# Four RMS norms split into their gain, applied to the turned block, and their root, applied to the product

## The chip, the cores and the metric

One Trainium2 chip, one of its cores. A time is device time in microseconds (us) for one launch of the whole program. The kernel before was timed three times: 2165.26, 2167.34 and 2168.16 us, median 2167.34. The profile is one further execution, recorded instruction by instruction.

The engines by their names in the profile: PE is the matrix engine (PEld its weight loads), DVE the vector engine, ACT the scalar engine, POOL the engine that here takes roots and issues indirect transfers, SP the one that issues most of the weight loads. Each engine runs its own list in order and waits for the others on semaphores. A float32 matmul goes through PE in two passes, so a matmul of the code is two in the profile's counts.

## What is computed

256 tokens of width 1024 pass through three layers. The parts that matter here:

```python
def rms_norm(x, g):
    y = x * lax.rsqrt(mean(x * x, axis=-1) + EPS)
    return y * g

# first block
h = rms_norm(x, norm_attn);  proj = h @ w_in            # then MLA and dilated attention
x = x + merged @ w_out
h2 = rms_norm(x, norm_ffn)
gp = softmax(h2 @ w_rg + b_rg)                          # 4 groups, the best one
el = h2 @ w_re + b_re                                   # 8 experts of it, the best two
x = x + sum(combine[e] * (silu(h2 @ w_gate[e]) * (h2 @ w_up[e])) @ w_down[e])   # 32 experts

# second block, layer 0 (layer 1 has a convolution in the place of the attention)
x = x + attn_retention_mixer(rmsnorm(x, norm_mix[0]), even_w_in, even_w_out)
t = rmsnorm(x, norm_ffn[0])
# peer: 8 heads, top 16 of 128 x 128 pairs of keys, per token 128 rows u and v of a table
s = (t @ w_q) . sub_keys;  x = x + sum_k gate_k * gelu(t . u[e_k]) * v[e_k]
```

Because a norm's root is one number per token and its gain one number per column of x, `rms_norm(x, g) @ W` equals `root * ((x * g) @ W)`.

## The kernel before, in words

Tokens lie in two chunks c of 128, one token per partition: `x[:, c, :]`, and normed in `xn[:, c, :]`. PE needs the width on the partitions, so a chunk is turned: eight 128x128 transposes into two banks of 512 columns (k = 0 and k = 4), each copied out to `hT`, k = 0 by ACT and k = 4 by DVE. A product is eight matmuls of 512 columns into one bank, four for each weight tile of 1 MiB. Weight tiles go through a ring of six slots, and later through places in the arena too; SP issues each load when the slot's last tile is used.

A norm takes four engines in turn: ACT squares and sums x (L394), DVE makes the mean (L398), POOL the root (L402), DVE multiplies x by root and gain in two halves (L417). Only then can PE turn the chunk (L360).

The program in order, with the places that the change touches:

1. **Start.** SP fetches both chunks of x and the identity, ACT the gain (512 KB, broadcast to all partitions). PE runs six filler matmuls on zeros (`pe_idle_work`, L369), turns chunk 0, runs four fillers, and begins `w_in` (L345, L314). The first attention stage follows.
2. **Residual and router** (`pe_residual`, `dve_residual`, `act_residual`, `vector_moe`). Four half products of 512 columns with `w_out` (L455): chunk 0, chunk 0, chunk 1, chunk 1. Chunk 0 is normed and turned beside the third half, chunk 1 after the fourth. `router` (L1412) multiplies a turned chunk by 36 router columns; `choose(c)` is a chain of small DVE instructions (L1492 to L1533) that ends in `Ms(c)`, the tokens' two experts as ones; a matmul with a triangle (L1434, L1439) ranks the tokens of each expert; `whose_tile` and `whose_place` make a table, and DVE writes the rows' numbers (`to_rows`, L1585, L1587). ACT stores the normed rows in `h_rows` (L1682). POOL gathers them by that table (L1348).
3. **Experts.** Sixteen tiles, six weight tiles of 1 MiB each; 19 places hold weights in advance. Each place is loaded again when PE has used it (L1205).
4. **Even layer.** DVE adds the experts' rows to x (L1673), the chunk is normed (`mix0`), turned, and multiplied by seven slabs of 512 columns (L1824) in the order 0, 512, 1536, 2048, 1024, 2560, 3072, with attention and retention between them, then by `even_w_out` (L1915). This is chunk 0; four slabs of chunk 1 follow, the rest of it lies inside the next stage.
5. **Peer stages.** Chunk 0 is normed (`ffn20`), turned and scored (L2334), DVE chooses the first head's 16 rows, and POOL issues 512 indirect gathers (L2818) of 128 rows of 8 KB, five ahead of their use. DVE takes the dot product of each (L2716), ACT makes a diagonal matrix of its weights (L2783), and PE adds the second half of the rows through it (L2702). The rest of chunk 1's even layer, the odd layer, and all later norms are spread between these positions by a table of positions.

## Time and profile before

| what | us |
|---|---|
| median of three runs | 2167.34 |
| lowest, highest | 2165.26, 2168.16 |
| the profiled execution: its span, first to last instruction | 2168.7 |
| PE busy in it | 1855.1 |
| DVE busy | 1305.5 |
| POOL busy | 687.5 |
| ACT busy | 493.1 |

The page gives no time for the profiled execution beside its span. The span lies 1.4 us above the median and 0.5 us above the highest of the runs. Differences of stages are read inside the span and taken off the median.

In the page's second part each digit is the busy share of one fortieth of the span (54 us), in tenths. PE is busy nearly everywhere in the first third. The DMA engines are busy from slice 8 on, except in slices 11 and 13, which hold the change from the experts to the even layer and the beginning of the peer stage.

### The profile page before, as it was taken

The page shows a single profiled execution, that of the slowest core. Times are in us where ns is not written, and L with a number is a line of the kernel's source. Part 1 is how long each engine was busy: PE and PEld are TensorE (multiplying, and loading weights), DVE is VectorE, ACT ScalarE, POOL GpSimd, SP SyncE. Part 2 cuts the span into 40 slices and gives each one's busy share as a digit, 9 for nine tenths or more (in the row PEclk, how much of TensorE's full clock was granted, in tenths as well). Part 3 has the DMA queues.
Part 4 walks back from the last instruction along what each step waited for, and adds up shares of the span by engine and source line. Part 5 has one row for each costly group of instructions (what it writes and reads, how often), then busy time and mean ns, then how long its engine had stood idle before and what let it go on. Part 6 is the DMA issues. An engine that isn't in the chain of part 4 may idle for free.

```text
span 2168.7 us, 19290 instructions
## 1 busy us (share of the span) xinstructions
PE 1855.1 (86%) x5992; PEld 893.5 (41%) x5992; DVE 1305.5 (60%) x3327; ACT 493.1 (23%) x1232; POOL 687.5 (32%) x593
## 2 busy tenths in 40 slices
PE   9999999998799989999877787777888767878875
PEld 4445555333245445455433333333433433434332
DVE  1343433221033668667587797987777898777764
ACT  1232221111022233222221122222212222222221
POOL 2110001111000334344343344453434444444442
PEclk9999999999999999999998998889999988999999
DMA  7432367999795999999999999999999999999996
GB/s 250 168 122 81 128 271 249 415 418 419 293 385 201 395 390 374 422 420 421 421 422 421 420 399 415 422 416 421 421 421 421 392 409 416 422 421 421 421 410 259
DMA packets 115081, 781.44 MB, mean 360 GB/s; under 512 B 16080, under 2 KB 17792, under 8 KB 21664
## 3 DMA queue, kind: packets, MB, share of 16 engines
q0 software_dynamic: 78928, 542.37, 60.9%
q1 hardware_dynamic: 32544, 227.75, 26.4%
q10 hardware_dynamic: 3504, 10.04, 1.2%
q8 instruction: 50, 0.82, 0.2%
q14 instruction: 55, 0.45, 0.1%
HBM read 782.20 MB, written 10.49 MB: 366 GB/s over the span
## 4 chain that ended last, share of the span: by engine, by line
DMA 29%; DVE 17%; issue 14%; POOL 6%; PE 5%; ACT 0%; POOLq 0%; DVEq 0%; ACTq 0%
DMA arena<-in_c_rows_dram,arena 29%; DVE arena L2716 7%; POOL arena L2818 6%; PE banks L1824 2%; DVE x L2726 2%; PE banks L2702 1%; DVE arena L2610 1%; DVE arena L2613 1%; DVE arena L2619 1%; PE banks L1915 1%; DVE arena L2648 1%; DVE arena L2652 0%; DVE arena L2577 0%; DVE small L2607 0%; DVE xn L417 0%
## 5 line engine op out<-in xcount | busy, mean ns | idle before, releaser
L2702 PE MATMUL banks<-arena 128*128 128x512 f32 x1784 | 885.4, 642 | 240.0 <-ACT arena L2783 239.1
L2818 POOL DMA_INDIRECT arena<-in_c_rows_dram,arena x512 | 609.7, 1191 | 817.5 <-PE banks L2702 571.3
L2716 DVE CUSTOM_DVE_ANT_0 arena<-arena,xn 128x1024 f32<-128x1024 f32 x512 | 625.4, 1223 | 296.9 <-DMA arena<-in_c_rows_dram,arena 294.2
L2702 PEld LDWEIGHTS banks<-arena 128*128 128x128 f32 x1784 | 345.8, 203 | 714.2 <-issue 356.6
L2783 ACT ACTIVATE arena<-ident,small 128x128 f32<-128x128 f32 x446 | 158.2, 395 | 536.6 <-DVE small L2723 524.7
L314 PE MATMUL banks<-ring,hT 128*128 128x512 f32 (+1 forms) x480 | 202.2, 577 | 0.0
L376 ACT COPY arena<-banks 128x512 f32<-128x512 f32 (+4 forms) x218 | 101.2, 493 | 292.5 <-PE banks L360 112.7
L2774 ACT ACTIVATE small<-small 128x2 f32<-128x2 f32 x256 | 52.1, 204 | 499.1 <-DVE small L2716 498.9
L402 POOL TENSOR_TENSOR small<-small 128x1 f32<-128x1 f32 (+4 forms) x24 | 33.5, 1398 | 303.3 <-DVE small L398 276.9
L314 PEld LDWEIGHTS banks<-ring,hT 128*128 128x128 f32 x480 | 87.9, 191 | 100.1 <-issue 98.4
L2407 PE MATMUL banks<-ring,hT 128*128 128x512 f32 x176 | 88.3, 606 | 0.0
L2726 DVE SCALAR_TENSOR_TENSOR x<-arena,small,x 128x1024 f32<-128x1024 f32 x66 | 84.9, 1286 | 2.4
L381 DVE COPY arena<-banks 128x512 f32<-128x512 f32 (+1 forms) x35 | 23.6, 675 | 96.4 <-PE banks L1269 67.4
L2450 PEld LDWEIGHTS banks<-hT,ring 128*128 128x128 f32 x448 | 62.5, 197 | 33.4 <-issue 33.4
L1250 PE MATMUL banks<-arena 128*64 128x512 f32 x280 | 71.6, 596 | 2.9 <-DMA arena<-in_c_experts_dram 2.9
L1362 POOL DMA_INDIRECT y_rows<-arena x16 | 16.0, 1001 | 183.0 <-ACT arena L376 99.8
L1327 DVE TENSOR_TENSOR arena<-arena,banks 128x256 f32<-128x256 f32 x16 | 6.7, 422 | 103.9 <-ACT arena L1299 103.9
L1824 PE MATMUL banks<-ring,hT 128*128 128x512 f32 x144 | 63.6, 592 | 0.0
L2450 PE MATMUL banks<-hT,ring 128*128 128x128 f32 x448 | 62.9, 280 | 0.0
L360 PEld LDWEIGHTS banks<-ident,arena 128*128 128x128 f32 (+1 forms) x416 | 47.3, 140 | 31.1 <-issue 28.3
L610 DVE SCALAR_TENSOR_TENSOR arena<-arena,banks 128x128 f32<-128x128 f32 (+1 forms) x64 | 19.7, 350 | 66.0 <-PE banks L554 66.0
L360 PE MATMUL banks<-ident,arena 128*128 128x128 f32 (+1 forms) x416 | 55.3, 275 | 2.1 <-DVE arena L1327 1.5
(319 smaller groups left out, 1805.3 us busy)
## 6 DMA issues: line engine op xcount, KB each, us to landing
arena<-in_c_experts_dram SPq DMA_DIRECT2D x51, 1024.0 KB, 21.5
ring<-in_c_w_in_dram SPq DMA_DIRECT2D x30, 1024.0 KB, 4.8
ring<-in_c_experts_dram SPq DMA_DIRECT2D x30, 1024.0 KB, 24.9
ring<-in_c_odd_w_in_dram SPq DMA_DIRECT2D x19, 1024.0 KB, 9.8
ring<-in_c_w_q_dram SPq DMA_DIRECT2D x18, 1024.0 KB, 9.6
ring<-in_c_even_w_in_dram SPq DMA_DIRECT2D x12, 1024.0 KB, 19.2
arena<-in_c_even_w_in_dram SPq DMA_DIRECT2D x10, 1024.0 KB, 15.4
arena<-in_c_rows_dram,arena POOLq DMA_INDIRECT x512
```

The costliest lines, as they stand in the source:

```text
L314: r = e.matmul(banks[:, b, 0:n], lhs[:, k + i, c * P:(c + 1) * P], wt[:, i, :], start=(k + i == 0), stop=(k + i == kn - 1))
L360: r = e.transpose(banks[0:m, b, i * P:(i + 1) * P], s, ident[:, :])
L376: e.copy(dst, src).then_inc(ac.sem, ac.up(name))
L1250: r = e.matmul(banks[H * h:H * h + H, b, :], gT[:, n % 2, 4 * part + k, H * h:H * h + H], wt[h][:, k, :], start=(part == 0 and k == 0), st ...
L1824: r = e.matmul(banks[:, bank_of[name], :], hT[:, k + i, c * P:(c + 1) * P], wt[:, i, :], start=(k + i == 0), stop=(k + i == 7))
L2407: r = e.matmul(banks[:, bank_of[name], :], hT[:, k, c * P:(c + 1) * P], wt[:, k % 4, :], start=(k == 0), stop=(k == 7))
L2450: r = e.matmul(banks[:, bank_of[name], f * P:(f + 1) * P], wt[:, k, f * P:(f + 1) * P], hT[:, k, c * P:(c + 1) * P], start=(k == 0), stop= ...
L2702: r = e.matmul(banks[:, bank_of[("acc", L, c, hf)], :], diag[:, diag_of[m], :], rows[:, row_of[m], D + hf * 512:D + (hf + 1) * 512], start ...
L2716: e.tensor_tensor_reduce(u, u, xn[:, c, :], 1.0, 0.0, ALU.mult, ALU.add, hid3[:, c, h, k:k + 1]).then_inc(ve.sem, ve.up(("u", p)))
L2726: e.scalar_tensor_tensor(x[:, c, :], rows[:, row_of[p - 1], D:2 * D], hid3[:, c, h, k + 1:k + 2], x[:, c, :], ALU.mult, ALU.add).then_inc( ...
L2783: e.activation(diag[:, diag_of[m], :], ident[:, :], ACT.Copy, scale=hid3[:, c, h, k:k + 1]).then_inc(ac.sem, ac.up(("diag", m)))
L2818: e.indirect_dma_start(rows[:, b, :], None, table_uv, bass.IndirectOffsetOnAxis(ap=eix[:, c, 16 * h + k:16 * h + k + 1], axis=0)).then_inc ...
```

## The change

The norms `attn`, `ffn`, `mix0` and `ffn20` are split. Three later norms stay as they were.

- PE turns x itself (`pe_turn_half`). The gain lies in a small tensor, one column per block of 128 (`c_gains`, 16 KB), and is multiplied in while the turned block is copied out: one DVE instruction for four blocks with a broadcast (`dve_gained`), or four ACT instructions with a scale operand (`act_gained`).
- The root multiplies what comes out of the product, as a scale in ACT's copy (`act_rooted`) or in DVE's. The router's logits get it in `scalar_tensor_tensor`.
- In the residual stage chunk 0 is turned in the middle of the third half product, the router's first matmuls run before the fourth, `choose(0)`, its table and its rank run beside the fourth. The normed rows for `h_rows` are still needed: DVE multiplies x by the gain, ACT by the root.
- At the end of the experts the three fillers before the turn go. In the even layer the score of the first two heads stands ahead of chunk 1's first product, of which the first half stood ahead of the turn before.
- The identity is fetched before x, and the broadcast gains of `attn` and `mix0` are no longer fetched.

```diff
+        def pe_turn_half(e, n, c, k):
+            turn(e, ("hT", n, c, k), [x[:, c, (k + i) * P:(k + i + 1) * P] for i in range(4)])
+        def act_gained(e, n, c, k):
...
+            for i in range(4):
+                e.activation(hT[:, k + i, c * P:(c + 1) * P], banks[:, bank_of[name], i * P:(i + 1) * P], ACT.Copy,
+                             scale=gain_T[n][:, k + i:k + i + 1]).then_inc(ac.sem, ac.up(name))
+        def dve_gained(e, n, c, k):
...
+            e.tensor_tensor(hT[:, k:k + 4, c * P:(c + 1) * P], turned(name, P, 4),
+                            gain_T[n][:, k:k + 4].unsqueeze(2).to_broadcast([P, 4, P]),
+                            ALU.mult).then_inc(ve.sem, ve.up(name))
+        def await_root(e, n, c):
+            e.wait_ge(po.sem, po.at(("ms", n, c)))
+        def act_rooted(e, name, dst, src, n, c):
+            await_root(e, n, c)
+            e.wait_ge(pe.sem, pe.at(name))
+            e.activation(dst, src, ACT.Copy, scale=ssn[n][:, c:c + 1]).then_inc(ac.sem, ac.up(name))
...
-            a2 = half(1, 0)
+            a2 = half(1, 0, first_turned)
             rings.drop(a2)
-            pe_turn_chunk(e, n, 0, xn[:, 0, :])
-            mid0(e)
-            a3 = half(1, 512)
-            mid1(e)
+            router(e, 0)
+            a3 = half(1, 512, ranked)
             rings.drop(a3)
-            pe_turn_chunk(e, n, 1, xn[:, 1, :])
+            turn_added(e, 1, 0)
+            turn_added(e, 1, 4)
+            router(e, 1)
...
+            def square(c):
+                e.wait_ge(ve.sem, ve.at(("res" + n, 512, "c", c)))
+                e.activation(scratch, x[:, c, :], ACT.Square,
+                             accum_out=ssn[n][:, c:c + 1]).then_inc(ac.sem, ac.up(("sq", n, c)))
+            def normed(c):
+                await_root(e, n, c)
+                e.wait_ge(ve.sem, ve.at(("xg", n, c)))
+                e.activation(xn[:, c, :], xn[:, c, :], ACT.Copy,
+                             scale=ssn[n][:, c:c + 1]).then_inc(ac.sem, ac.up(("xn", n, c)))
+                store(e, c)
             e.wait_ge(ve.sem, ve.at(("res" + n, 512, "c", 0)))
             free(e)
+            square(0)
+            act_gained(e, n, 0, 0)
+            normed(0)
+            act_gained(e, n, 1, 0)
+            chain(e, ac)
+            square(1)
+            normed(1)
...
         def vector_first(e):
             e.memset(hT[:, 0:2, :], 0.0).then_inc(ve.sem, ve.up("zeros"))
+            e.wait_ge(pe.sem, pe.at(("idle", "x")))
+            dve_gained(e, "attn", 0, 0)
             for c in range(2):
-                dve_norm(e, "attn", c)
-            for c in range(2):
-                dve_turned_chunk(e, "attn", c)
+                e.wait_ge(ac.sem, ac.at(("sq", "attn", c)))
+                dve_mean(e, ssn["attn"][:, c:c + 1], D, ("ms", "attn", c))
+            dve_gained(e, "attn", 1, 0)
...
-                step(e.tensor_tensor(g8[:, 0:4], banks[:, b, 0:4], rb[:, 0:4], ALU.add))
-                step(e.tensor_tensor(l, banks[:, b, 4:36], rb[:, 4:36], ALU.add))
+                step(e.scalar_tensor_tensor(g8[:, 0:4], banks[:, b, 0:4], root, rb[:, 0:4], ALU.mult, ALU.add))
+                step(e.scalar_tensor_tensor(l, banks[:, b, 4:36], root, rb[:, 4:36], ALU.mult, ALU.add))
...
-            await_hT(e, "mix0", 1)
-            pe_even_in(e, 1, 0, 0)
-            pe_turn_chunk(e, "ffn20", 0, xn[:, 0, :])
+            for c0, k in ((0, 0), (512, 4)):
+                e.wait_ge(ve.sem, ve.at(("joined", 0, c0)))
+                pe_turn_half(e, "ffn20", 0, k)
             await_hT(e, "ffn20", 0)
             pe_score(e, 0, 0, (0,))
             pe_score(e, 0, 1, (0,))
-            pe_even_in(e, 1, 0, 4)
+            e.wait_ge(ve.sem, ve.at(("hT", "mix0", 1, 0)))
+            e.wait_ge(ac.sem, ac.at(("hT", "mix0", 1, 4)))
+            both(1, 0)
             both(1, 512)
...
             for i in range(2):
                 e.wait_ge(ys_out[i].sem, ys_out[i].at("all"))
             pe_idle_work(e, "results", 8, still)
-            e.wait_ge(ve.sem, ve.at(("x", "mix0", 0)))
-            pe_idle_work(e, "results added", 3, still)
             tensor_even(e)
```

On PE the residual and router stage, before. The matmuls on `ring,hT` are the half products, those on `small,hT` the router, those on `small` alone fillers; the last row is the first rank.

```order
L455 MATMUL banks<-ring,hT 128x512 x16
L360 MATMUL banks<-ident,xn 128x128 x8
L455 MATMUL banks<-ring,hT 128x512 x8
L1412 MATMUL banks<-small,hT 128x36 x8
L369 MATMUL banks<-small 128x288 x4
L360 MATMUL banks<-ident,xn 128x128 x8
L1412 MATMUL banks<-small,hT 128x36 x8
L1434 MATMUL banks<-arena,small 128x32
```

The same place on PE in the changed kernel:

```order
L490 MATMUL banks<-ring,hT 128x512 x12
L361 MATMUL banks<-ident,x 128x128 x8
L490 MATMUL banks<-ring,hT 128x512 x4
L1489 MATMUL banks<-small,hT 128x36 x8
L490 MATMUL banks<-ring,hT 128x512 x4
L1503 MATMUL banks<-arena,small 128x32
L490 MATMUL banks<-ring,hT 128x512 x4
L361 MATMUL banks<-ident,x 128x128 x8
L1489 MATMUL banks<-small,hT 128x36 x8
```

The turn moved into the third half product, the router ahead of the fourth, the rank into its middle, and the four fillers are gone.

On PE the change from the even layer's chunk 0 to the scores, before. L1915 is the last product of chunk 0, L1824 are chunk 1's products, L2334 the queries and L2346 their scores.

```order
L1915 MATMUL banks<-arena,hT 128x512 x8
L1824 MATMUL banks<-arena,hT 128x512 x4
L360 MATMUL banks<-ident,xn 128x128 x8
L2334 MATMUL banks<-hT,arena 128x128 x16
L2346 MATMUL banks<-arena 128x128 x2
L2334 MATMUL banks<-hT,arena 128x128 x16
L2346 MATMUL banks<-arena 128x128 x2
L1824 MATMUL banks<-arena,hT 128x512 x28
```

And in the changed kernel:

```order
L1985 MATMUL banks<-arena,hT 128x512 x8
L361 MATMUL banks<-ident,x 128x128 x8
L2412 MATMUL banks<-hT,arena 128x128 x16
L2424 MATMUL banks<-arena 128x128 x2
L2412 MATMUL banks<-hT,arena 128x128 x16
L2424 MATMUL banks<-arena 128x128 x2
L1894 MATMUL banks<-arena,hT 128x512 x32
```

Four matmuls of chunk 1 moved from before the turn to behind the scores.

## Rows read from the trace of the kernel before

**Rows 1.** The page: busy tenths of the DMA engines in 40 slices.
```profile
DMA  7432367999795999999999999999999999999996
```

**Rows 2.** Instructions in time, start: start us, us, engine, line, operation.
```profile
1.46 7.43 PE L369 MATMUL banks<-hT 128*128 128x512 f32 x12 [1.46 <-DVE hT L910]
...
11.17 1.02 PE L345 MATMUL banks<-ring,hT 128*128 128x512 f32 x2
```

**Rows 3.** Longest wait of PE from 15 to 325 us: total, times, longest.
```profile
PE banks L554 <- ACT arena L376: 1.8, 2, 1.0
```

**Rows 4.** Instructions in time, router stage.
```profile
345.97 1.87 PE L1412 MATMUL banks<-small,hT 128*128 128x36 f32 x16
...
348.31 0.56 POOL L402 TENSOR_TENSOR small<-small 128x1 f32<-128x1 f32 x1 [14.06 <-DVE small L398]
...
350.47 0.34 ACTq L1682 DMA_DIRECT2D h_rows<-xn  x1
...
354.32 0.16 DVE L1492 TENSOR_TENSOR arena<-banks,small 128x4 f32<-128x4 f32 x1
...
357.32 0.19 DVE L1533 TENSOR_TENSOR arena<-arena 128x32 f32<-128x32 f32 x1
...
362.42 0.17 DVE L1587 TENSOR_SCALAR arena<-arena 128x16 uint32<-128x16 uint32 x1
...
363.52 1.17 POOL L1348 DMA_INDIRECT arena<-h_rows,arena  x1 [14.66 <-issue]
...
369.10 1.04 PE L360 MATMUL banks<-ident,arena 128*128 128x128 f32 x8
```

**Rows 5.** Line L1682, the stores of h_rows.
```profile
DMA to landing us min/median/max: 6.8/7.0/7.3
```

**Rows 6.** Line L1348, the gathers of h_rows, 360 to 372 us.
```profile
DMA to landing us min/median/max: 3.3/3.5/3.7
```

**Rows 7.** Stretches: us, engines busy, granted clock, DMA share, GB/s.
```profile
360.00:365.00 5.00, 3.86 (x10) 3.04 (x11) 1.60 (x14) 1.45 (x8) 1.17 (x2) 0.55 0.91 374
370.00:375.00 5.00, 5.00 (x30) 2.41 (x30) 0.69 (x1) 0.32 (x1) 0.99 (x1) 1.00 0.09 26
500.00:510.00 10.00, 7.10 (x30) 2.55 (x27) 1.09 (x2) 1.06 (x3) 0.00 (x0) 0.83 1.02 418
720.00:740.00 20.00, 18.16 (x43) 7.83 (x42) 19.00 (x55) 6.63 (x15) 6.99 (x6) 1.00 1.01 418
```

**Rows 8.** Instructions in time, beginning of the even layer.
```profile
606.72 1.06 ACT L394 ACTIVATE xn<-x 128x1024 f32<-128x1024 f32 x1 [15.76 <-DVE x L1673]
...
611.88 3.60 PE L1824 MATMUL banks<-ring,hT 128*128 128x512 f32 x8
```

**Rows 9.** The chain that ended last, even layer: slab 1024 of chunk 0.
```profile
642.96 6.87 PE banks L1824 x16
```

**Rows 10.** Line L275, issues of SP from 608 to 608.7 us.
```profile
L275 SPq DMA_DIRECT2D ring<-in_c_even_w_in_dram x2: 446/570/695, 607.8 to 608.6; - x2
...
DMA to landing us min/median/max: 12.2/12.2/12.2
```

**Rows 11.** Line L275, issues of SP from 610.4 to 611 us.
```profile
L275 SPq DMA_DIRECT2D arena<-in_c_even_w_out_dram x2: 442/463/484, 610.1 to 610.6; - x2
...
DMA to landing us min/median/max: 23.3/23.3/23.3
```

**Rows 12.** Instructions in time, beginning of the peer stage.
```profile
683.31 0.69 DVE L2042 TENSOR_TENSOR x<-x,banks 128x512 f32<-128x512 f32 x1 [2.74 <-PE banks L1915]
...
689.05 3.81 PE L2334 MATMUL banks<-hT,arena 128*128 128x128 f32 x32 [0.83 <-ACT hT L376]
...
705.66 1.03 POOL L2818 DMA_INDIRECT arena<-in_c_rows_dram,arena  x1 [19.67 <-DVE arena L2668]
...
716.87 1.22 DVE L2716 CUSTOM_DVE_ANT_0 arena<-arena,xn 128x1024 f32<-128x1024 f32 x1 [3.02 <-DMA arena<-in_c_rows_dram,arena]
```

**Rows 13.** Instructions in time: a pair of 128x128 ACTIVATEs with a scale operand.
```profile
740.51 0.69 ACT L2783 ACTIVATE arena<-ident,small 128x128 f32<-128x128 f32 x2 [1.14 <-DVE small L2723]
```

More of the change, by code:

```diff
@@ L442, in sp_residual, with pe_residual, half @@
                     load(e, ("res" + n, c0, k), w[c0 // 256 + k // 4])
-        def pe_residual(e, n, lhs, second, mid0, mid1, ready):
-            def half(c, c0):
+        def pe_residual(e, n, lhs, second, ready, router, ranked):
+            def half(c, c0, between=None):
                 name = ("res" + n, c0, "c", c)
@@ L483, in add, with times_gain, mean @@
                 emptied[name] = (ve.sem, ve.n)
+            def times_gain(c, c0):
+                g = fetched("gain_" + n)
+                e.wait_ge(g.sem, g.at("all"))
+                chain(e, ve)
+                e.tensor_tensor(xn[:, c, c0:c0 + 512], x[:, c, c0:c0 + 512], gain[:, gain_of[n], c0:c0 + 512],
+                                ALU.mult).then_inc(ve.sem, ve.up(("xg", n, c)))
+            def mean(c):
+                e.wait_ge(ac.sem, ac.at(("sq", n, c)))
+                dve_mean(e, ssn[n][:, c:c + 1], D, ("ms", n, c))
@@ L494, in dve_residual, with act_residual @@
-            mid1(e)
-            dve_turned_chunk(e, n, 1)
-        def act_residual(e, n, mid0, mid1, free):
+            dve_gained(e, n, 1, 4)
+            mean(1)
+            times_gain(1, 512)
+        def act_residual(e, n, store, free):
+            def square(c):
[8 more added lines that the diff above has]
+                store(e, c)
@@ L1006, in scalar_first @@
         def scalar_first(e):
-            gain_fetch(e, "attn")
+            g = fetched("gains")
+            e.dma_start(gT_all, a["c_gains"]).then_inc(g.sem, g.up("all", by=16))
             for c in range(2):
@@ L1414, in router @@
                 r.then_inc(pe.sem, pe.up(("lg", c)))
-            def first_router(e):
-                router(e, 0)
-                pe_idle_work(e, "norm", 4, still)
-            still = rw.rearrange("p k n -> p (k n)")
-            pe_residual(e, "ffn", hT, second, nothing, first_router, ready)
-            router(e, 1)
-            rings.drop(("lg", 0))
-            rings.drop(("lg", 1))
             def bank(name):
@@ L1428, in bank, with ranked @@
                 return b
-            b = bank(("rank", 0))
-            e.wait_ge(fetched("tri").sem, fetched("tri").at("all"))
-            e.wait_ge(po.sem, po.at("ones"))
-            e.wait_ge(ve.sem, ve.at(("Ms", 0)))
-            e.matmul(banks[:, b, 0:32], tri, Ms[:, 0, :], start=True, stop=True).then_inc(pe.sem, pe.up(("rank", 0)))
+            def ranked(e):
+                b = bank(("rank", 0))
+                e.wait_ge(fetched("tri").sem, fetched("tri").at("all"))
+                e.wait_ge(po.sem, po.at("ones"))
+                e.wait_ge(ve.sem, ve.at(("Ms", 0)))
+                e.matmul(banks[:, b, 0:32], tri, Ms[:, 0, :], start=True, stop=True).then_inc(pe.sem, pe.up(("rank", 0)))
+            still = rw.rearrange("p k n -> p (k n)")
+            pe_residual(e, "ffn", hT, second, ready, router, ranked)
+            rings.drop(("lg", 0))
+            rings.drop(("lg", 1))
             b = bank(("rank", 1))
@@ L1561, in whose_place, with chosen @@
                                          ALU.is_equal, ALU.mult), ("hots", c))
-            first = choose(0)
-            def some(n):
-                for _ in range(n):
-                    next(first, None)
-            dve_residual(e, "ffn", lambda e: some(3), lambda e: some(5))
-            for _ in first:
-                pass
-            e.wait_ge(po.sem, po.at("ids"))
-            whose_tile(0)
+            def chosen(e):
+                for _ in choose(0):
+                    pass
+                e.wait_ge(po.sem, po.at("ids"))
+                whose_tile(0)
+            dve_residual(e, "ffn", chosen, lambda e: whose_place(0))
             for _ in choose(1):
                 pass
-            whose_place(0)
             whose_tile(1)
@@ L2105, in scalar_even @@
         def scalar_even(e):
[L2106 removed]
+            act_gained(e, "mix0", 1, 4)
             past(e, "moe", pe, ve, po)
```

130 lines of the change are left out of this document (80 added, 50 removed).

## The prediction, made before the change was run

> **What bounds the kernel now.** I read the page first. Its DMA line [rows 1] shows the transfers busy from slice 8 to the end but for slices 11 and 13, so the experts and the peer stages run at the pace of the transfers, and the first attention stage, slices 1 to 6, does not. The list of waits, asked for PE from 15 to 325 us, has nothing longer than 1.8 us in all [rows 3]: the first stage runs at the pace of PE, and what its beginning gains is kept. Then the instructions in time at the four norms. What one of them gives depends on what comes due behind it, so each is followed until a transfer or PE takes over.
>
> **The start.** PE works at fillers until 1.46 + 7.43 = 8.89 us and begins the first product at 11.17 [rows 2]. Now x itself is turned, so PE turns as soon as the fillers end, and no earlier, since they stay. Eight transposes take at most 1.04 us, the last row of [rows 4], the four small fillers behind them as much, and the copy-out is beside these. The product starts at 10.6 to 11.0: 0.2 to 0.5 us gained, I take 0.4. ACT's half as four instructions costs more than one copy: a pair takes 0.69 [rows 13], so four some 1.3 us against 0.6, but PE needs that half only after the first half's product. The identity ahead of x costs nothing, since x is now awaited until 8.9. POOL's small transfers are issued later, because the mean of chunk 1 waits behind DVE's and ACT's turned blocks. I price that at nothing: they first serve angles and the small norms, while PE works off products, and what they delay at most is DVE, not PE.
>
> **The router.** Before, the fourth half product ends at 345.97, where the router begins [rows 4]. Now the router of chunk 0 (1.87, but for its overlap 1.7) and the rank (0.3) come ahead of that end: 348.1. `Ms(0)` must be there when PE has done the first half of the fourth product. The chain from L1492 to L1533 takes 3.2 us (354.32 to 357.51) and the four matmuls 3.4, so PE stalls 0.2 at most. What is queued behind that wait is the rest of the product, and behind it all of chunk 1. From 348.1: DVE adds (0.69, as in rows 12), ACT copies the turned block out in four, until 350.1, then squares (1.06 plus reading its sum, 1.25), mean and root take 0.9 (POOL's part 0.56), so the root is there at 352.2, and the router's product at about 352.0. `choose(1)` starts at 352.3 instead of 354.32. The chain of it is 3.2 again, and the whole of chunk 0's table, 1.2 us of `whose_place`, no longer stands behind it. The table's numbers were ready at 362.42 + 0.17 = 362.6; now at about 359.1, 3.5 earlier.
>
> That gain isn't all kept. The store of chunk 1's rows was issued at 350.47 [rows 4] and is now behind the square, the root and a multiplication by ACT (about 1.1): 353.4. Stores took 6.8 to 7.3 us to land [rows 5], so 360.2 to 360.7, later than the table. The first gather follows 0.9 behind the later of both (as 363.52 behind 362.6), at 361.3, and lands after 3.3 to 3.7 [rows 6], at 364.8. The two loads that wait for the same store are issued with it and share the transfers; I add 0.4. Before, the first gather landed at 363.52 + 3.7 = 367.2, but PE turned its rows only at 369.10: it was at its nine fillers, at a clock of 0.55 [rows 7]. If the clock is low there again, PE is free at 366.3 (359.1 and the same 7.2 us), if not at 365.2. I take 366.0, 3.1 us gained. The ends are 2.0 (POOL's 363.52 against 361.3, less some contention) and 3.9. From here on the gain is kept: at 370 to 375 the transfers stand still (share 0.09) until PE frees the first place, then run at a share of 1.02 (500 to 510 us) [rows 7] to the end of the experts.
>
> On the contention the Trainium skill ("DMA: Bandwidth & Descriptors", Queues, rings and completion order) says that a DMA engine takes packets from its queues in turn. By that the gather does not stand behind 2 MiB of weights; behind them it would come about 5 us later, and this norm would lose 1 to 2 us. The trace agrees with taking turns: the store issued at 350.47 landed within 7.3 us with a load of 1 MiB issued just ahead.
>
> **The even layer's beginning.** x is complete where ACT begins its square, 606.72, and the first product begins at 611.88 [rows 8], 5.2 us later. Now: turn 1.04, four small fillers 1.04, so 608.8, 3.1 earlier; the turn of chunk 1 waits for no norm, which gives 0.7 more. The removed 512 KB of gain and the three fillers are only room. But this is lost again at slab 1024. Its tile is the twelfth that SP asks for after the experts' results have landed. The fourth, issued at 607.8, landed 12.2 us later, 620.0 [rows 10], the ninth, issued at 610.6, 23.3 us later, 633.9 [rows 11]: 2.8 us a tile, so the twelfth lands at about 642.2 (an estimate). PE uses it at 642.96 [rows 9]. The transfers do not start earlier relative to the results, so of 3.8 us only 0.3 to 0.8 is left; I take 0.5. PE then stands still there for about 3 us.
>
> **The scores.** From the end of the last product of chunk 0 (683.1) to the first query matmul (689.05) [rows 12] are 5.9 us, 3.4 of them covered by a product of chunk 1. Now the wait is DVE's add (0.7 + 0.2), a half turned (0.6) and ACT's or DVE's copy-out (0.9): 2.5 us. The choice of the first rows and the first gather (705.66) come 3.4 us earlier, and 3.9 with the tile's 0.5. But the covering product, 3.4 us, is now behind the scores, so all later products of chunk 1 come only 0.5 earlier, and with them three things: the slots that the second to fifth gathers wait for, and the loads that wait for the same slots. From 720 to 740 the transfers have a share of 1.01 and DVE works 19 of 20 us [rows 7]. DVE's first dot product (716.87) may come 3 us earlier, the following ones wait for their rows. I give this stage 0.3 more than PE's shift. The bounds are 0 and 3.4. Scale operands in later ACT copies cost some 0.1 us each on an engine that is a quarter busy, and count nothing.
>
> **Sum.** 0.4 + 3.1 + 0.5 + 0.3 = 4.3 us off the span of 2168.7, and as much off the median of the runs, 2167.34: 2163.0. The likeliest case's own range is 2161 to 2165.
>
> **Rivals.**
> - *The choice decides the peer stage.* The critical chain goes through the first gather and DVE (716.87 is on it). If these decide, and not transfers and PE, the end moves by all 3.9: 0.4 + 3.1 + 3.9 = 7.4, 2160.0. For it: DVE is at 95%. Against: the transfers' 1.01 in the same stretch.
> - *The clock.* The new wait ahead of slab 1024 is 3 us. In the experts' stage PE waits for weights, and the granted clock is 0.83 from 500 to 510, which is 1.7 us of PE lost [rows 7]. If PE falls to its lower level (1.2 GHz) there and again between the turn and the scores, 2 x 1.7 = 3.4 are lost: 2166.4. The Trainium skill ("TensorE: Matmul & The Clock Gate", Why this matters for your kernels) advises against idle gaps between bursts of matmuls for this reason, and so speaks against taking out the fillers; by it this case would be the likely one. The trace is of two minds: it shows the low clock after such waits, but also at 360 to 365 among fillers.
> - *The router's gain is hidden.* The store lands as late as it can and the gather behind the loads: 1 us left of 3.1: 2165.1.
> - *Slower: the peer stage meets another phase.* From 740 to 860 PE, DVE and transfers are all near their limits and take turns in waiting. The product that moved behind the scores makes PE the one that frees the slots late, and each late slot keeps a gather back. The place is the first three heads of chunk 0; the price is 3.4 us of PE, twice if the scores of the next heads come late as well. It decides once more than 4.3 us of transfer time stands empty there in addition: 6.8 - 4.3, 2169.9.
>
> **Numbers.** What a measurement of this kernel tells from no change is about 0.2%, 4.3 us, so the forecast lies on the edge. Chances: forecast 0.42 (half of it below 2163.0), choice 0.18, clock 0.15, router hidden 0.15, slower 0.10. Faster by over 0.2%: 0.21 + 0.18 and the parts of the others in which two gains meet (the first stage's clock can differ by 1.7 as well), 0.11: 0.50. Within 0.2%: 0.42. Slower by over 0.2%, above 2171.7: only the last rival at its worst, 0.08. The range leaves out the far end of the last two: 2158.5 to 2167.5.
>
> **What would show it.** The first product at 10.6 to 11.0. `Ms(0)` there when the fourth product is half done; the first gather of h_rows behind the store's landing, not behind the table; PE turning its rows about 3 us earlier. A wait of PE for a transfer ahead of slab 1024, which the profile before does not have. The first query matmul about 4 us earlier, chunk 1's products about 0.5 (all counted beyond the router's 3.5). I am wrong if slab 1024 finds its tile there, if the gather waits for the table, or if from 860 us on the peer positions are earlier by more than 6 or less than 3 us.

## The result and the profile after: slower by 0.19%, where 0.2% faster was forecast

| kernel | median us | runs | ratio to before, 95% interval |
|---|---|---|---|
| before | 2167.36 | 20 | |
| changed | 2170.60 | 20 | 1.0019, 1.0010 to 1.0027 |

The forecast was 2163.0, within 2158.5 to 2167.5. The changed kernel lies 3.2 us above the kernel before by the medians (0.15%), outside the range and on the other side.

The profiled execution of the changed kernel has a span of 2165.7 us; its run took 2167.46, near the low end of the 20 (2166.74 to 2179.34). That of before, 2168.7, lies above the median of its kernel: in every recorded run the time is about 1.8 us longer than the span, so it stands for about 2170.5 (an estimate). One pair of profiles therefore says the opposite of 20 runs of each kernel, and the places below are read from several profiles of each.

The start, instructions in time, changed kernel (against [rows 2]):

```profile
1.46 7.32 PE L370 MATMUL banks<-hT 128*128 128x512 f32 x12 [1.46 <-DVE hT L980]
...
8.61 1.04 PE L361 MATMUL banks<-ident,x 128*128 128x128 f32 x8
...
10.38 3.60 PE L346 MATMUL banks<-ring,hT 128*128 128x512 f32 x8
```

The turn follows the fillers at once and the first product is 0.79 us earlier in this profile.

The router stage (against [rows 4]; L1489 is the router, L1567 the beginning of `choose`, L1657 the last of the table's numbers, L1755 the store of h_rows, L1282 SP's loads of experts' weights, L1425 the gather, L361 the turn):

```profile
344.27 3.68 PE L490 MATMUL banks<-ring,hT 128*128 128x512 f32 x8
...
351.90 0.22 DVE L1567 SCALAR_TENSOR_TENSOR arena<-banks,small 128x4 f32<-128x4 f32 x1
...
353.07 0.33 ACTq L1755 DMA_DIRECT2D h_rows<-xn  x1
...
358.72 0.18 DVE L1657 TENSOR_SCALAR arena<-arena 128x16 uint32<-128x16 uint32 x1
358.94 0.33 SPq L1282 DMA_DIRECT2D hT<-in_c_experts_dram  x1
359.39 0.36 SPq L1282 DMA_DIRECT2D xn<-in_c_experts_dram  x1
359.82 1.17 POOL L1425 DMA_INDIRECT arena<-h_rows,arena  x1 [8.19 <-DMA h_rows<-xn]
...
367.42 1.09 PE L361 MATMUL banks<-ident,arena 128*128 128x128 f32 x8 [1.83 <-DMA arena<-h_rows,arena]
```

Everything up to the gather's issue is as early as forecast or earlier: `choose(1)` at 351.9 (forecast 352.3), the table at 358.9 (359.1), the gather at 359.82 (361.3), 3.7 us before that of [rows 4]. The store of h_rows took 5.9 us here, not 6.8 to 7.3 [rows 5]: it landed at 358.9 too, so the gather did not stand behind the store as forecast. Then it takes 7.6 us until PE can turn the rows, and PE waits for them.

What moved meanwhile, from two answers on the DMA queues of the changed kernel, 360 to 363.9 us and 364 to 368 (packets, MB, share of the 16 engines; q1 carries SP's loads, q0 POOL's gathers):

```profile
q1 hardware_dynamic: 183, 1.37, 90.5%
```
```profile
q1 hardware_dynamic: 92, 0.62, 37.7%
q0 software_dynamic: 432, 0.48, 33.7%
```

For 4.3 us after the gather's issue no packet of it moves; SP's two loads, issued 0.9 and 0.4 us ahead of it, do. In the profile before the first packet moved 1.7 us after the issue, so 2.6 us of the 4.3 are new. In [rows 4] the two loads were issued at 357.81 and 358.63, 5 us ahead of the gather, which then landed in 3.3 to 3.7 us [rows 6].

The even layer's beginning (ACT's loads of the experts' results, L1772 here, then SP's loads of weights, which wait for them). Before, with the product of slab 1024:

```profile
599.07 0.82 ACTq L1700 DMA_DIRECT2D arena<-y_rows  x2
...
606.41 2.60 SPq L275 DMA_DIRECT2D ring<-in_c_even_w_in_dram  x5
...
642.79 7.03 PE L1824 MATMUL banks<-ring,hT 128*128 128x512 f32 x16
```

Changed:

```profile
595.47 0.81 ACTq L1772 DMA_DIRECT2D arena<-y_rows  x2
...
604.09 2.46 SPq L276 DMA_DIRECT2D ring<-in_c_even_w_in_dram  x5
...
606.34 3.60 PE L1894 MATMUL banks<-ring,hT 128*128 128x512 f32 x8
...
639.25 7.39 PE L1894 MATMUL banks<-ring,hT 128*128 128x512 f32 x16 [1.36 <-DMA ring<-in_c_even_w_in_dram]
...
652.58 3.70 PE L1894 MATMUL banks<-ring,hT 128*128 128x512 f32 x8 [1.19 <-DMA ring<-in_c_even_w_in_dram]
```

The first product is 5.5 us earlier than in [rows 8]: 3.6 come from the result loads, which are issued that much earlier, and 1.9 are gained between the two, where the forecast had 3.1. From the issue of the result loads to SP's first load behind them it takes 8.6 us where it took 7.3, and PE waits for weights twice, at slab 1024 as forecast and again in slab 2560. From the issue of the result loads to the end of chunk 0's last join it takes 86.1 us, before 84.2.

The second profile of the changed kernel (`e1_after`, see below) looks different at slab 1024. The first row is its product, the second the stretch from 642 to 645 us (us, engines busy, granted clock, DMA share, GB/s); the third is the same stretch of before:

```profile
640.62 8.80 PE L1894 MATMUL banks<-ring,hT 128*128 128x512 f32 x16 [2.91 <-DMA ring<-in_c_even_w_in_dram]
```
```profile
642.00:645.00 3.00, 3.00 (x5) 1.28 (x4) 1.48 (x4) 0.00 (x0) 0.00 (x0) 0.51 1.00 410
```
```profile
642.00:645.00 3.00, 3.00 (x15) 1.80 (x14) 1.80 (x4) 2.22 (x4) 0.00 (x0) 1.00 1.01 412
```

After a wait of 2.9 us PE runs this product for 3.4 us at its lower level, 1.2 GHz, and needs 8.80 us for it instead of 7.03.

### The profile page after: what moved, and what is told of

It reads as the page before. It is cut to its first block, busy times and chain, and to the rows that moved or that the text cites. A ratio compares the mean times of both kernels' runs of the same rounds, so it can differ in the third digit from the quotient of the medians.

```text
span 2165.7 us, 19328 instructions
## 1 busy us (share of the span) xinstructions
PE 1844.2 (85%) x5978; PEld 887.9 (41%) x5978; DVE 1301.6 (60%) x3320; ACT 503.0 (23%) x1254; POOL 678.6 (31%) x593
## 4 chain that ended last, share of the span: by engine, by line
DMA 33%; DVE 15%; issue 13%; POOL 5%; PE 5%; ACT 0%; POOLq 0%; DVEq 0%; ACTq 0%
DMA arena<-in_c_rows_dram,arena 32%; DVE arena L2796 7%; POOL arena L2898 5%; DVE x L2806 2%; DMA ring<-in_c_even_w_in_dram 1%; PE banks L2782 1%; PE banks L1894 1%; DVE arena L2690 1%; DVE arena L2693 1%; PE banks L370 1%; DVE arena L2699 1%; PE banks L2412 1%; PE banks L1985 1%; DVE arena L2728 1%; DVE arena L2732 1%
## 5 line engine op out<-in xcount | busy, mean ns | idle before, releaser
L2898 POOL DMA_INDIRECT arena<-in_c_rows_dram,arena x512 | 600.8, 1173 | 826.5 <-PE banks L2782 544.0
L377 ACT COPY arena<-banks 128x512 f32<-128x512 f32 (+4 forms) x185 | 83.6, 478 | 191.9 <-PE banks L361 111.6
L382 DVE COPY arena<-banks 128x512 f32<-128x512 f32 x32 | 22.1, 690 | 86.5 <-PE banks L1346 66.4
L361 PEld LDWEIGHTS banks<-ident,arena 128*128 128x128 f32 (+1 forms) x416 | 47.1, 140 | 34.5 <-issue 26.9
L361 PE MATMUL banks<-ident,arena 128*128 128x128 f32 (+1 forms) x416 | 55.5, 275 | 5.0 <-DMA arena<-h_rows,arena 1.8
```

What stands on the lines that cost most here:

```text
L361: r = e.transpose(banks[0:m, b, i * P:(i + 1) * P], s, ident[:, :])
L377: e.copy(dst, src).then_inc(ac.sem, ac.up(name))
L2898: e.indirect_dma_start(rows[:, b, :], None, table_uv, bass.IndirectOffsetOnAxis(ap=eix[:, c, 16 * h + k:16 * h + k + 1], axis=0)).then_inc ...
```

## Where the time lies, over all profiles

Each experiment below was profiled too, and most share their code with one of the two kernels at the places that matter. So each place can be read several times. Shifts are us against the first profile of before (negative is earlier). The dot products are counted from 0, and the place is the beginning of number 48.

| stretch | text before | text changed |
|---|---|---|
| the restart: the experts' first load behind the gathers | 0, -0.3, 0.0 | -1.6, -1.6, -0.7, -0.1, -2.6, +0.6, +1.1, -1.9: mean -0.9 |
| result loads to the last join, us | 84.2, 84.3, 84.2 | 86.1, 86.6, 86.7, 86.5, 86.6, 86.6: +2.3 |
| last join to first query matmul, us | 5.8 | 2.3: -3.4 |
| first query to dot product 48, us | 175.2, 171.3, 172.5 | 175.6, 176.5, 176.7: +3.3 |
| dot product 48 to the end, us | 1304.5, 1304.8, 1304.6 | 1306.2, 1304.5, 1306.9: +1.2 |

The sum, -0.9 + 2.3 - 3.4 + 3.3 + 1.2, is +2.5; the medians of the 20 runs differ by 3.2. About 0.7 us has no place in this table. Two limits of it: the first row takes eight profiles and the last three rows only three, whose spans alone are 1.1 us longer on the mean than the three of before; and over all twelve profiles with the split of `mix0` the last row is +0.6 rather than +1.2.

The row from the result loads to the last join hides two things that come and go:

- *A packet of PE's instructions among the results' last packets.* In the seven profiles that have one 5.0 to 5.7 us after ACT's issue, SP's first load follows that issue by 8.6 to 8.8 us. In the eleven others it follows by 7.3 to 7.5.
- *The clock at slab 1024.* PE waits there in all twelve profiles with the split of `mix0`, and in none of the six without it. In eight of the twelve the clock then falls to its lower level for 3.4 us and the product takes 8.6 to 8.8 us instead of 7.0 to 7.4. Whether it falls is not settled by the length of the wait: it fell after 2.0 us and did not after 2.65.

| | clock falls at slab 1024 | it does not |
|---|---|---|
| packet among the results | 86.5, 86.6, 86.6, 86.6 | 86.1, 86.7 (a second wait, in slab 2560); 84.3 (ACT's loads later) |
| no packet | 85.7, 85.7, 85.5, 85.8 | 84.0 |

The numbers are us from the result loads to the last join; without the split it is 84.2 or 84.3 in all six. ACT's loads are later in the 84.0 too and in the last three of the left lower cell. So the fall of the clock costs about 1.7 us (85.7 against 84.0), and the packet 0.8 to 0.9 beside it (86.5 and 86.6 against 85.7). The second wait is long only where the clock doesn't fall and PE is at slab 2560 sooner.

## The experiments

**The kernels again, and parts undone.** `e1_before` and `e1_after` are the two kernels unchanged. `e1_noS` takes the norm `ffn20` and its order back; its core:

```diff
-            for c0, k in ((0, 0), (512, 4)):
-                e.wait_ge(ve.sem, ve.at(("joined", 0, c0)))
-                pe_turn_half(e, "ffn20", 0, k)
+            pe_even_in(e, 1, 0, 0)
+            pe_turn_chunk(e, "ffn20", 0, xn[:, 0, :])
```

`e1_onlyF` is the kernel before with the diff's `pe_residual`, `dve_residual`, `act_residual`, `choose` and what they call, and nothing else.

> The kernel before, unchanged, for a second profile. All theories: its median within 2 us of 2167.4. If the spread of its runs comes from the peer stage, then its 160th dot product lies elsewhere than 1194.3 us, by up to 3 us, while the join of the even layer ends at 683.1 within 0.5.

> The changed kernel, unchanged, for a second profile: 2170.6 within 2 us. Theory 'lost in the peer stage': its query matmul at 683.9 as in the first profile, and the 16th to 160th dot products later than in that one by 2 to 6 us. Theory 'lost earlier': the query matmul itself comes later than 683.9 by 2 us or more in a typical run.

> The changed kernel with the norm ffn20 and the order around its turn as before (the first half product of chunk 1 ahead of the turn, norm, turn, scores). Theory 'the product that moved behind the scores puts the peer stage into a worse phase': 2165 to 2167, 4 to 6 below the changed kernel. Theory 'the loss comes from another norm': within 1.5 of the changed kernel, 2169 to 2172.

> The kernel before with the split of ffn and the reordered router alone; attn, mix0 and ffn20 as before. Theory 'the router gain is real and kept': 2164 to 2166, 1.7 to 3 below before. Theory 'the router is where it is lost' (the experts' transfers or the clock in them): 2169 to 2171.

Measured: before 2168.92 (12 runs, ratio 0.9998 to 1.0024), changed 2169.70 (1.0001 to 1.0023), without the split of `ffn20` 2170.91 (1.0008 to 1.0030), router alone 2168.37 (0.9991 to 1.0012). Undoing `ffn20` gives nothing back, so the loss isn't the product that moved behind the scores; the router alone gains nothing that can be measured. The first query of the changed kernel, at 683.9 in its first profile, is at 685.5 in the second and 686.8 in the third (`e4_after`): the first profile was early there. The second profile of before differs from the first by 3.8 us at the end and by 0.3 at the join: its gain lies between the first gather and dot product 48, so a peer stage alone varies by that much with one text.

**Three causes, one edit each, and all together.** In `e2_gather_first` SP's loads into hT and xn also wait for the first gather:

```diff
             elif s in (XN_AT, HT_AT):
+                e.wait_ge(xg_in[0].sem, xg_in[0].at(("xg", 0)))
                 e.wait_ge(fetched("h_rows").sem, fetched("h_rows").at("all"))
```

In `e2_code_moved` the fillers behind the experts are `[still] * 4 + [still[:, 0:P]] * 16` instead of eight `still`. In `e2_act_later` four loads, the two gains and those of kt and cw, move in ACT's program:

```diff
-            gain_fetch(e, "ffn20")
-            gain_fetch(e, "mix1")
-            g = fetched("kt0")
...
             act_even_out(e, 0, 2560)
+            gain_fetch(e, "ffn20")
+            gain_fetch(e, "mix1")
+            g = fetched("kt0")
```

> The changed kernel, but SP's two 1 MiB loads that wait for the store of h_rows (into hT and xn) also wait until the first gather of h_rows has landed. Theory 'the gather stands behind these two loads': the first gather lands 3.3 to 3.7 us after its issue instead of 7.2 to 8.5, PE turns its rows 1.5 to 2.5 us earlier relative to the gather's issue, the stretch after it is at full clock, and everything behind is 1.5 to 3 us earlier: about 2168. Rival 'a gather issued within a microsecond of the table is slow by itself': the landing stays over 6 us and the time at 2170.

> The changed kernel, with the eight filler matmuls of 512 columns at the end of the experts as four of 512 and sixteen of 128 columns: same length, 48 instructions more on PE (with the weight loads), so that PE's next code packet (16 KB) is fetched earlier. Theory 'that packet holds up the last rows of the experts' results on one of the 16 DMA engines': the packet is fetched before 597 us, the second result load lands 7.3 us after its issue instead of 8.7, and the even layer's weights come 1.3 us earlier: 2169. Rival 'it lands late because nothing follows it in its queue': 8.7 stays, 2170.5.

> The changed kernel, with ACT's loads of two gains, the keys and the convolution (2.1 MB) issued behind its copy-out of slab 2560 instead of at the beginning of the even layer. Theory 'these loads, now issued 1 to 1.6 us earlier against the weights, take the share of slab 2560': the second tile of 2560 arrives up to 3 us earlier, PE's wait there goes and the last join of chunk 0 ends 1.5 to 2 us earlier against the results' arrival: 2168.5 if it is kept. Rival 'weights alone saturate the queues': no change, 2170.5.

> The three edits together. If they add: first gather landed within 3.7 us, results landed within 7.4, no wait at slab 2560, so the first query matmul is 4 to 6 us earlier than in the changed kernel. If the peer stage passes on what comes before it: 2165. If it gives none of it on (the transfers decide from there): 2170.

Measured, 12 runs each, against before: gather first 2164.51 (0.9976 to 0.9999); code moved 2167.43 (0.9994 to 1.0015); ACT later 2168.90 (0.9995 to 1.0019); all three 2162.13 (0.9971 to 0.9996).

With the gather first, line L1426, 355 to 372 us, and the instructions there:

```profile
DMA to landing us min/median/max: 3.3/4.5/7.2
```
```profile
359.87 1.17 POOL L1426 DMA_INDIRECT arena<-h_rows,arena  x1 [8.29 <-DMA h_rows<-xn]
...
363.27 0.33 SPq L1283 DMA_DIRECT2D hT<-in_c_experts_dram  x1
...
365.36 1.04 PE L361 MATMUL banks<-ident,arena 128*128 128x128 f32 x8
```

The first gather lands in 3.4 us, the loads then go out, and at the restart nothing is seen of their delay, since they only filled the gap that follows. The transfers of the experts start 3.7 us earlier than before instead of 0.9 on the mean, and 3.1 of it are left at the result loads. (In the same answer for the changed kernel, 358 to 368 us, the three values are 5.5, 6.3 and 7.6.) The time fell by more than the 3 us forecast, to 2164.5 where 2168 was expected; its profile, with a span of 2166.4, doesn't show where.

All profiles say the same of the gather. In the nine in which it goes out with the two loads its first packet moves 3.6 to 4.7 us after the issue and it lands after 7.2 to 9.5. In the nine in which it has 5 us of distance to them or goes first, these are 1.7 and 3.4 to 3.7. The rival, that a gather issued just behind the table is slow by itself, is out. What holds its packets back (the DMA engines, or the making of its descriptors) isn't shown.

PE's clock adds to it. Stretches (us, engines busy, granted clock, DMA share, GB/s) of `e4_noA`, a later run with the same router text, in which fillers ran at full clock, were done at 361 us and PE then waited 6.9 us for the gather; then of all three edits:

```profile
360.00:365.00 5.00, 1.31 (x6) 0.70 (x4) 0.00 (x0) 0.00 (x0) 2.00 (x2) 1.00 1.00 370
365.00:370.00 5.00, 1.76 (x8) 1.76 (x9) 0.00 (x0) 0.59 (x1) 0.00 (x0) 0.55 0.27 99
370.00:375.00 5.00, 5.00 (x25) 3.04 (x26) 0.69 (x1) 0.00 (x0) 0.99 (x1) 0.77 0.10 26
```
```profile
360.00:365.00 5.00, 4.34 (x29) 3.44 (x29) 0.69 (x1) 0.58 (x1) 2.79 (x4) 1.00 0.53 117
365.00:370.00 5.00, 5.00 (x24) 1.63 (x24) 0.00 (x0) 0.00 (x0) 0.56 (x1) 1.00 0.97 386
```

After the long wait PE turns the rows and does the first expert's products at its lower level, 1.2 GHz; the eight transposes take 1.97 us instead of 1.09. This is why an earlier gather could end in a later restart (+0.6, +1.1 us in the table): in the four profiles in which the clock is low for 6.8 us behind that wait, the restart is at -0.7, -0.1, +0.6 and +1.1; in the five others with the loads beside the gather, router alone among them, it is at -0.8 to -2.6. With all three edits together PE turned the rows at 361.5 to 362.9 at full clock in four profiles of four, and the restart came 6.1 to 7.5 us earlier than before. The fillers ran at full clock there and at the lower one in `e2_gather_first`; no edit aims at that, and why isn't known.

With the code moved, the queues' answers. First the changed kernel, 595.4 to 604.2 us, then `e2_code_moved`, 596.5 to 604.5 us:

```profile
q10 hardware_dynamic: 288, 2.10, 63.0%
q8 instruction: 1, 0.02, 0.7%
...
arena<-y_rows ACTq DMA_DIRECT2D x2, 1024.0 KB, 6.5
```
```profile
q10 hardware_dynamic: 288, 2.10, 69.1%
issues: line engine op xcount, KB each, median us to landing
arena<-y_rows ACTq DMA_DIRECT2D x2, 1024.0 KB, 5.8
```

One packet of instructions, 16 KB, runs from 601.2 to 602.2 us in the changed kernel. Fifteen of the sixteen last packets of the results have come by 602.3. A chain of three more packets of 8 KB begins at 602.2, where that of the instructions ends, and the sixteenth comes at 603.6; SP, which waits for it, issues at 604.09. Between the two almost nothing moves (DMA share 0.04):

```profile
602.20:603.40 1.20, 1.20 (x4) 0.50 (x3) 0.88 (x1) 0.00 (x0) 0.00 (x0) 1.00 0.04 14
```

In `e2_code_moved` the packet came at 595.8 and SP's loads began at 603.88, 7.3 us after ACT's at 596.59. In the kernel before it came at 613.5. To the last join it now took 85.7 us instead of 86.1 to 86.7, although the clock fell at slab 1024. The runs gained more than this 1 us explains (2167.4 against 2170.6), which the spread between series allows.

With ACT's loads later the second tile of slab 2560 lands 51.0 us after the issue of the result loads instead of 57.1, the wait there is gone, and the last join is back at 84.3 us after them, though the code packet is still there. But the clock did not fall in that profile. In three of the four with all edits it fell and the join came at 85.5 to 85.8, so the 84.3 isn't the edit's alone. The tile came at 51.0 in all of them. Nor was the earlier issue of ACT's loads enough to make it late: with the code moved they went out just as early (15.9 us after the result loads), and the tile came at 54.5, as in the kernel before (54.6). The profile of `e2_act_later` lost its gain again: it had the worst restart but one (+0.6) and 179.8 us from the query to dot product 48. So that this edit pays by itself isn't shown by its runs; that it removes the wait is.

**What the norms are worth.** `e3_noM` takes the split of `mix0` back in the changed kernel (the norm, its turn, the copies with a root, the three fillers). `e3_router_gather` is `e1_onlyF` with the edit of `e2_gather_first`. `e3_all_order` is all three edits with

```diff
+            pe_even_in(e, 1, 0, 0)
             for c0, k in ((0, 0), (512, 4)):
...
-            both(1, 0)
+            pe_even_in(e, 1, 0, 4)
```

and `e3_all_noS` all three edits with `ffn20` as in `e1_noS`.

> The changed kernel with the norm mix0 as before (gain fetched as one row, x multiplied by root and gain, three fillers ahead of the turn). Theory 'the split of mix0 costs more than it gives': from the issue of the result loads to the end of chunk 0's last join it takes 84.2 us as in the kernel before instead of 86.1 to 86.7, and the time is 1.5 to 2.5 below the changed kernel. Rival 'it costs nothing there': 86 or more, and the time as the changed kernel's.

> The kernel before with the split of ffn and the reordered router alone, and SP's two loads waiting for the first gather. Theory 'the router gives its 3 us once the gather is alone': the transfers of the experts start again 3 to 3.7 us earlier than in the kernel before, and the time is 3 to 4 below it, 2163 to 2164.5. Rival 'PE's fillers and its low clock keep it': 0 to 1.5 earlier, 2166 to 2167.

> All three edits, and the first half product of chunk 1 ahead of the turn and the scores again (the norm ffn20 stays split). Theory 'chunk 1's products and the transfers set the pace, not the scores': from the last join to the 48th dot product 178 to 180 us as with the scores first, time within 1.5 of 2162.5. Rival 'the scores first are worth their 3.4 us': 3 us slower.

> All three edits, with the norm ffn20 and the order around it as before. Theory 'the split of ffn20 is worth nothing': within 1.5 of 2162.5. Rival 'it is worth its 3.4 us once the stages ahead are mended': 2165 to 2166. Rival 'it costs': below 2161.

Measured: without the split of `mix0` 2169.13 (1.0008 to 1.0026), and 84.3 us to the last join, as expected; the code packet no longer falls into the result loads either. Only about 1 us of the 2.3 shows in the median. Router alone with the gather first 2166.85 (0.9986 to 1.0007): the experts' transfers start 3.1 us earlier, 3.1 are left at the result loads, and the stretch from the join to dot product 48 was 181.6 us instead of 177 to 181. The place is as the theory said, the time as the rival said. Product ahead of the scores again 2163.12 (0.9976 to 0.9997), 1.0 above the first result of all three and 2.6 above the second. From the join to dot product 48 it took 181.8 us, where 178 to 180 was expected and the two profiles of all three have 177.9 and 178.3. So the place speaks for a worth of 3.5 to 3.9 us and the time for less; one profile doesn't settle it. Without the split of `ffn20` 2165.04 (0.9985 to 1.0006): 2.9 above the first result of all three, while its profile, 2158.8, is the shortest of all. Between nothing and 3 us this isn't settled.

**One more series.**

> The kernel before, unchanged, in one series with the changed kernel. All theories: the experts' transfers start again within 0.3 us of the first profile's place, and from the issue of the result loads to the last join it takes 84.2 to 84.4 us. Theory 'the split as a whole costs about 1.5 us': 1 to 2 us faster than e4_after; theory 'it costs about 3': 2.5 to 4 faster.

> The changed kernel, unchanged, in one series with the kernel before. The experts' transfers start again between 2.6 earlier and 0.6 later than before, as in the five profiles of this router code so far; 86.1 to 86.7 us from the result loads to the last join; 5.2 minus 1.8 to 3 us at the first query matmul.

> The changed kernel with the norm attn and the start as before. Theory 'the start's 0.8 to 1 us is kept to the end of the attention stage, but lost at the gather, which is as late as the loads beside it make it': the router begins 0.8 to 1.2 us later than in the changed kernel, the transfers start again in the same band, and the time is within 1 of it. Rival 'the start is the part that pays': 1 us slower.

> The three edits together a second time, as the version that should beat both: 2161 to 2164, 3 to 5 below the kernel before of this series and 6 to 8 below the changed kernel. If its first result was luck: 2165 or more.

`e4_noA` has the diff's parts for the start undone. Measured: before 2166.82 (12 runs), changed 2172.16 (9 runs, ratio 1.0013 to 1.0033), without the split of `attn` 2171.35 (1.0004 to 1.0024), all three again 2160.50 (6 runs, 0.9957 to 0.9980). The last is the version that beats both kernels, by some 4 to 7 us the kernel before and 8 to 12 the changed one. Before and changed differ by 5.3 us here, more than either theory had (1 to 2, or 2.5 to 4), and by 0.8 in the first series: one series of 12 doesn't size this difference. The start's part makes no difference that can be measured; its router began 0.35 us later than in `e4_after`, not 0.8 to 1.2.

## Why the prediction was wrong, step by step

In the forecast's own terms the sum was 0.4 + 3.1 + 0.5 + 0.3 = 4.3 us gained. The router, with what was left of the start, gave 0.9 instead of 3.5, the even layer lost 2.3 instead of gaining 0.5, the scores gave about nothing, and the rest, which had no term, lost 0.6 to 1.2.

- **The start** was right at its place: the first product came 0.8 us earlier in the first profile, and over the twelve profiles with the new start 0.6 on the mean (9.9 to 11.3 against 11.2), where 0.4 was forecast. How much is kept isn't settled. Among the profiles with the changed router its matmuls of chunk 1 begin at 349.3 to 350.2 where the clock was low for 3.4 us at about 29 us, and at 348.2 to 349.0 where it was not. In the first group the new start is ahead by 0.6 us, in the second by nothing. "What its beginning gains is kept" is thus shown in part only.
- **The router** failed in one step: "lands after 3.3 to 3.7 [rows 6], at 364.8. The two loads that wait for the same store are issued with it and share the transfers; I add 0.4." PE turned the rows 7.2 to 9.6 us after the gather's issue in nine profiles (5.3 to 5.6 in three of before). [Rows 6] was taken at a moment when the two loads had been under way for 5 us; the change brought the gather and the loads together, and the loads won. So 3.3 to 3.7 plus 0.4 was mis-sized: the landing took 7.2 to 9.5. The rule of the Trainium skill that I set beside it ("DMA: Bandwidth & Descriptors", Queues, rings and completion order: a DMA engine takes packets from its queues in turn) is not what shows here: nothing of the gather moved for 3.6 to 4.7 us, where 1.7 is its own delay. The row I took as agreement was a store against a load, both issued by hardware queues, and says nothing on a gather. "About 5 us later", which I had written for the other case, is near what came (about 4 to 6 later). It was also the rival "The router's gain is hidden" (1 us left of 3.1), by its second half: the gather behind the loads, but not a late store. With the start's share taken off, even less was left on the mean.
- **The clock** was a rival with a chance of 0.15, and its first half came true: the wait ahead of slab 1024 was there in all twelve profiles with the split (forecast about 3 us), and in eight of them the clock fell behind it, at 1.7 us each, the price that I had given it. Of the changed kernel's own three profiles one shows the fall, of its variants seven of nine; the first profile, with 1.4 us of waiting and no fall, is not the usual case. The second half did not come: the clock stayed full between the turn and the scores. A further fall came behind the wait for the gather, a place where I had put PE at its fillers.
- **The even layer** failed in "The transfers do not start earlier relative to the results, so of 3.8 us only 0.3 to 0.8 is left; I take 0.5". The twelfth tile did land where I had put it, 43.3 to 44.2 us after the result loads in every profile (before 43.4), and PE used it 43.4 to 44.4 us after them, before 43.7 to 43.9: a gain of 0.4 at the most, and a loss of up to 0.6 in some. What failed is that I followed the stage no further than this tile, and left out the clock behind the wait. Three things came on top: the fall of the clock (1.7 us, in eight of twelve); SP's loads, which started 1.3 us later because the second result load landed later behind a packet of PE's instructions (0.8 to 0.9 at the join); and, where the clock did not fall, a second wait in slab 2560 (1.2 and 1.7 us), whose second tile landed 56.7 to 57.7 us after the result loads instead of 54.6. ACT's own loads, to which I gave no term, share the queues then: with four of them moved away the tile lands at 51.0. Instead of a gain of 0.5 there was a loss of 2.3.
- **The scores** were right: the query matmul 3.4 us earlier against the join, and chunk 1's products not. The change gains nothing there (0.3 forecast), since what was gained at the query is paid back up to dot product 48; with `ffn20` as before the query comes 5.8 us behind the join and that stretch takes 172.5 us, as in the third profile of before.
- **The rest**, to which I gave nothing, lost 0.6 to 1.2 us. What does it isn't known. I had written that I am wrong if from 860 us on the positions are not at least 3 us earlier: dot product 48 begins 0.1 us earlier on the mean of three profiles of each. The rival on the other side (the peer stage meets another phase, 3.4 us of PE, first three heads; its sum of 6.8 - 4.3 gives 2169.8, not 2169.9) names the right sign and nearly the time, but by luck: with that product put back, alone or on top of the three edits, the time does not fall.
- The forecast also leaned on one profile of before that was 3.0 and 3.8 us slower than the two others of the same text, nearly all of it in the peer stage. I noted the span against the median (1.4 us) and drew nothing from it.

## What to carry to other kernels

When a change brings a small transfer forward, list what else is issued at that new moment, above all what waits for the same signal; a landing time read where the small transfer was alone is a lower bound only. If the large loads only fill a gap, let them wait for the small one: here that one wait took the time from above the kernel before to just below it (2164.5 against 2166.4). Where a forecast puts a new wait on PE, give the clock behind it a term of its own. Where runs of one text differ by as much as the change, read each stretch from several profiles, relative to its own beginning, before explaining a total.

## What the runs showed that was not expected

- With two loads of 1 MiB issued 0.9 and 0.4 us ahead of an indirect gather of 128 rows no packet of it moved for 4.3 us, and it landed after 7.6; with the loads held back its first packet moved after 1.7 us and it landed after 3.4.
- PE's instructions are themselves fetched, 16 KB at a time, 50 times in the kernel, about 1 us each. One that falls into the last microseconds of a load delays its landing by 1.3 us. 48 more instructions ahead moved it from 601.2 to 595.8 us. The change as a whole had moved it from 613.5 to 601.2; with `mix0` undone it was at 612.0 again.
- Fillers that are short are no cover against a longer wait: at full clock nine fillers ended 2.7 us sooner than at the lower one (4.61 instead of 7.28 us), and PE then stood still for 6.9 us and came back at 1.2 GHz.
- The clock can fall behind a wait of 2.0 us and stay up behind one of 2.65 us, in the same place of nearly the same program.
